# Mixing tile 0 rounded, subtracted and half multiplied inside the latent stage of a hybrid encoder layer

## What is computed

```
ret_out = silu(rg) * groupnorm(retention(q, k, v))            # 8 heads x 64
mla_out = latent_attention(...)                                # 4 heads x 128
mix = concatenate([ret_out, mla_out], axis=-1)                 # (S, 1024)
x = x + einsum('bse,ed->bsd', mix, w_out)
x = x + hier_moe(rmsnorm(x, g_ffn), ...)   # top-1 of 4 groups, top-2 of 8 experts in it
y = rmsnorm(x, g_final)
```

## Time and profile before

| what | value |
|---|---|
| three runs | 1511.76, 1516.46, 1519.86 us |
| profiled execution, its own time | 1517.54 us |
| its span, first to last instruction | 1516.0 us |
| TensorE matmuls busy | 1401.2 us (92% of the span) |
| VectorE busy | 1085.1 us (72%) |
| ScalarE busy | 859.0 us (57%) |
| GpSimd busy | 391.7 us (26%) |
| mean granted clock of TensorE | 0.968 |
| data moved | 329.12 MB, 217 GB/s over the span |

### The profile page before, as it was taken

How to read it: one execution, slowest core, us unless ns; L and a number is a source line. 1 busy time by engine, 2 the same in 40 slices (tenths; PEclk the granted TensorE clock), 3 DMA queues, 4 the chain that set the end, 5 groups by cost and what they waited for, 6 DMA issues and landing times.

```text
span 1516.0 us, 23099 instructions
## 1 busy us (share of the span) xinstructions
PE 1401.2 (92%) x8472; PEld 1159.0 (76%) x8472; DVE 1085.1 (72%) x1526; ACT 859.0 (57%) x1029; POOL 391.7 (26%) x280
## 2 busy tenths in 40 slices
PE   5999899999988999996999769999999999999983
PEld 4788788888877788885888648888887777777771
DVE  4766776444457677772576678999988888888876
ACT  5644444333446555552444457777777777777764
POOL 2000111111133000000122232666643333334431
PEclk9999999999999999998999869999999999999997
DMA  8344422222121100014557548999999999999977
GB/s 275 113 158 144 151 83 72 83 84 84 63 84 50 56 29 29 29 42 155 189 213 277 192 180 320 391 384 393 389 391 383 384 367 372 370 381 378 377 275 294
DMA packets 63242, 329.12 MB, mean 217 GB/s; under 512 B 11862, under 2 KB 18406, under 8 KB 50882
## 3 DMA queue, kind: packets, MB, share of 16 engines
q1 hardware_dynamic: 45906, 278.60, 48.5%
q0 software_dynamic: 17264, 49.56, 10.8%
HBM read 285.06 MB, written 51.80 MB: 222 GB/s over the span
## 4 chain that ended last, share of the span: by engine, by line
PE 30%; DMA 14%; issue 4%; ACT 3%; DVE 3%; POOLq 0%; DVEq 0%; POOL 0%; SPq 0%; ACTq 0%
PE acc L96 9%; PE acc L98 9%; PE acc L97 9%; DMA plain<-in_w_gate 7%; DMA odd_gate<-in_w_gate 6%; ACT shared L1825 3%; PE acc L2470 1%; PE acc L2020 1%; PE acc L2440 1%; DMA s_h_rows<-plain 1%; DVE split L1830 1%; PE acc L2031 1%; DVE plain L2605 1%; DVE plain L2643 0%; DMA plain<-s_h_rows,plain 0%
## 5 line engine op out<-in xcount | busy, mean ns | idle before, releaser
L96 PE MATMUL acc<-shared,split 128*128 128x512 f32 x952 | 383.5, 403 | 16.0 <-DVE split L2088 10.3
L98 PE MATMUL acc<-shared,split 128*128 128x512 f32 x952 | 374.7, 394 | 0.0
L96 PEld LDWEIGHTS acc<-shared,split 128*128 128x128 f32 x952 | 181.3, 190 | 53.5 <-DVE split L2088 10.6
L1830 DVE TENSOR_TENSOR even_lo<-plain,shared 128x4096 fp32r<-128x4096 f32 x48 | 211.8, 4420 | 7.8 <-ACT shared L1825 6.6
L98 PEld LDWEIGHTS acc<-shared,split 128*128 128x128 f32 x952 | 180.9, 190 | 39.0
L96 PE MATMUL pa<-shared,a_xT_hi 128*128 128x512 f32 (+1 forms) x480 | 193.2, 403 | 16.0 <-DVE a_w_lo L736 14.9
L1825 ACT CAST shared<-plain 128x4096 fp32r<-128x4096 f32 x48 | 174.3, 3633 | 40.2 <-DMA plain<-in_w_up 15.9
L98 PE MATMUL pa<-shared,a_xT_lo 128*128 128x512 f32 (+1 forms) x480 | 186.7, 389 | 0.0
L97 PE MATMUL acc<-even_lo,split 128*128 128x512 f32 x384 | 150.7, 392 | 0.0
L1830 DVE TENSOR_TENSOR split<-odd_rest,shared 128x4096 fp32r<-128x4096 f32 x31 | 137.0, 4421 | 6.0 <-ACT shared L1825 5.8
L2335 POOL DMA_INDIRECT plain<-s_h_rows,plain x32 | 133.2, 4162 | 21.9 <-issue 12.2
(11 more groups left out here) (334 smaller groups left out, 2722.6 us busy)
## 6 DMA issues: line engine op xcount, KB each, us to landing
plain<-in_w_gate SPq DMA_DIRECT2D x16, 2048.0 KB
plain<-in_w_up SPq DMA_DIRECT2D x16, 2048.0 KB
plain<-in_w_down SPq DMA_DIRECT2D x16, 2048.0 KB
odd_rest<-in_w_down SPq DMA_DIRECT2D x16, 2048.0 KB
odd_gate<-in_w_gate SPq DMA_DIRECT2D x16, 2048.0 KB, 20.5
odd_rest<-in_w_up SPq DMA_DIRECT2D x16, 2048.0 KB, 21.3
a_x_turned<-in_x_turned SPq DMA_DIRECT2D x24, 512.0 KB, 3.5
a_x_row<-in_x SPq DMA_DIRECT2D x12, 512.0 KB, 4.9
```

Of the source, the lines that this page charges most:

```text
L96: pe.matmul(out, st_hi, mv_hi, start=first, stop=False)
L98: return pe.matmul(out, st_lo, mv_hi, start=False, stop=last)
L1830: eng.tensor_tensor(self.w_lo[half][m], self.raw[half][m][:, 0:4096], self.w_hi[m].bitcast(F32), ALU.subtract).then_inc(self.s_wlo[m], 1)
```

## The change

Tile 0 of the mixing stage is begun in the latent stage. An object `Ahead` holds places and semaphores that both programs use; its semaphores are not cleared between them.

- SyncE, after the load of output piece 3, waits for the first four stores and fetches `mixT[0]` and `x[0]`; ahead of the store of group 10 it fetches `mixT[1]`.
- GpSimd, once the scores of unit 39 are made, rounds `mixT[0]` and subtracts.
- TensorE makes half 0 of tile 0 in bank 6: pieces 4 to 7, 0 and 1 (18 matmuls) after the transposes of unit 45, pieces 2 and 3 (6 matmuls) before the last weighing. `split_mix(3)` moves ahead of unit 47's rounding on ScalarE and of its subtraction on VectorE.
- SyncE no longer waits for the stores at the end of the program; the wait is ahead of the fetch of tile 2 in the mixing stage.
- The mixing stage starts with half 1 of tile 0 (24 matmuls), without a wait. The addition of x for tile 0 is in two pieces of 512 columns. Tile 1's rounding and subtraction come first on ScalarE and VectorE.

```diff
+class Ahead:
+    def __init__(self, space, sem):
+        self.mx = [space.words("f_mx0", Space.ROPE, D), space.words("f_mx1", Space.TABS, D)]
+        self.xr = space.words("f_xr", Space.KEYS + 4 * TOK, D)
+        self.hi, self.lo = space.rounded("f_hi", Space.Q_HI, D), space.rounded("f_lo", Space.Q_LO, D)
+        self.product = space.bank(6)
...
@@ phase_latent, sync @@
             load_out(3)
+            for i in range(2):
+                sp.wait_ge(s_ost[i], 32)
+            sp.wait_ge(lat.s_rst, 16 * TILES)
+            sp.wait_ge(s_rot, 6)
+            sp.dma_start(ahead.mx[0], mixT[0]).then_inc(ahead.s_in[0], 16)
+            sp.wait_ge(s_clo, TILES)
+            sp.dma_start(ahead.xr, x_all[0]).then_inc(ahead.s_xr[0], 16)
             keep_out(5)
...
             load_out(7)
+            sp.wait_ge(s_s, 40)
+            sp.dma_start(ahead.mx[1], mixT[1]).then_inc(ahead.s_in[1], 16)
             keep_out(10)
             keep_out(11)
-            sp.wait_ge(s_ost[0], 16 * NG_ // 2)
-            sp.wait_ge(s_ost[1], 16 * NG_ // 2)
@@ gpsimd @@
             pool.wait_ge(lat.s_rst, 16 * TILES)
+            pool.wait_ge(s_s, 40)
+            pool.wait_ge(ahead.s_in[0], 16)
+            nc.gpsimd.tensor_copy(ahead.hi, ahead.mx[0]).then_inc(ahead.s_mhi, 1)
+            pool.wait_ge(ahead.s_mhi, 1)
+            nc.gpsimd.tensor_tensor(ahead.lo, ahead.mx[0], ahead.hi.bitcast(F32), ALU.subtract).then_inc(ahead.s_mlo, 1)
@@ tensor @@
+            def mix_first(ks):
+                for k in ks:
+                    if k == HM:
+                        pe.wait_ge(ahead.s_mlo, 1)
+                        pe.wait_ge(s_flo, 8)
+                    elif k < HM:
+                        pe.wait_ge(s_olo, HM + k + 1)
+                    rows = slice(k * P, (k + 1) * P)
+                    three_passes(pe, pz[:], ahead.hi[:, rows], ahead.lo[:, rows], out_piece(shared, OUT_HI, k, 0),
+                                 out_piece(shared, OUT_LO, k, 0), k == HM, k == HM - 1)
...
-                if u == NU - 2:
+                if u == NU - 3:
+                    mix_first((4, 5, 6, 7, 0, 1))
+                elif u == NU - 2:
                     weigh_last(0)
+            mix_first((2, 3))
             weigh_last(1)
@@ scalar @@
                 elif u == NU - 2:
                     split_mix(2)
+                    split_mix(3)
...
-            split_mix(3)
             take_out(NG_ - 1)
@@ phase_mix, sync @@
-            sp.dma_start(mx[:, 0, :], mixT[0]).then_inc(s_in[0], 16)
-            sp.dma_start(xr[:, 0, :], x_all[0]).then_inc(s_xr[0], 16)
...
                     if t:
+                        if t == 1:
+                            for i in range(2):
+                                sp.wait_ge(ahead.s_ost[i], 96)
                         sp.wait_ge(s_mlo, t)
-                    sp.dma_start(mx[:, 1 - half, :], mixT[t + 1]).then_inc(s_in[1 - half], 16)
-                    if t:
+                        sp.dma_start(mx(t + 1, 1 - half), mixT[t + 1]).then_inc(s_in[1 - half], 16)
                         sp.wait_ge(s_x2, t)
@@ tensor @@
-            for b in range(2):
-                project(0, 0, b, range(KD))
+            for k in range(KD):
+                rows = slice(k * P, (k + 1) * P)
+                ins = three_passes(pe, po[0][:, 512:1024], ahead.hi[:, rows], ahead.lo[:, rows],
+                                   out_piece(shared, OUT_HI, k, 1), out_piece(shared, OUT_LO, k, 1), k == 0, k == KD - 1)
+            ins.then_inc(s_po, 1)
             pe.wait_ge(s_const, 112)
@@ scalar @@
-            split(0, 0, 0)
             split(1, 0, 1)
@@ vector @@
-            split(0, 0)
+            split(1, 1)
             dve.wait_ge(s_const, 112)
...
             dve.wait_ge(s_tab[1], 16)
-            split(1, 1)
...
+                if isinstance(t, int) and t == 0:
+                    nc.vector.tensor_tensor(x2[:, 0, 0:512], ahead.product, ahead.xr[:, 0:512], ALU.add)
+                    nc.vector.tensor_tensor(x2[:, 0, 512:D], po[0][:, 512:D], ahead.xr[:, 512:D], ALU.add).then_inc(s_x2, 1)
```

More of the change, by code:

```diff
@@ L1105, in phase_latent @@
         s_pt, s_phi, s_plo = sem("pt"), sem("phi"), sem("plo")
-        s_o, s_oev, s_ost = sem("o"), sem("oev"), [sem("ost0"), sem("ost1")]
+        s_o, s_oev, s_ost = sem("o"), sem("oev"), ahead.s_ost
         groups = [(0, h, 0) for h in range(HM)] + [(1, h, b) for h in range(HM) for b in (1, 2)]
@@ L1831, in lower, with phase_mix @@
                           ALU.subtract).then_inc(self.s_wlo[m], 1)
-def phase_mix(nc, block, sems, shared, split, plain, acc, ex, mixT, x_all, g_ffn, w_rg, w_re, ident_d, route_d, blocks_d, x_mid,
+def phase_mix(nc, block, sems, shared, split, plain, acc, ex, ahead, mixT, x_all, g_ffn, w_rg, w_re, ident_d, route_d, blocks_d, x_mid,
               h_rows, table, s_tick, s_tock, w_exp):
@@ L1845, in phase_mix, with mx, xr @@
         x2, h_sb = place.at([P, 2, D], F32, 48 * KB), place.at([P, 2, D], F32, 56 * KB)
-        mx, xr = place.at([P, 2, D], F32, 64 * KB), place.at([P, 2, D], F32, 72 * KB)
+        mx_places, xr_places = place.at([P, 2, D], F32, 64 * KB), place.at([P, 2, D], F32, 72 * KB)
+        def mx(t, half):
+            return ahead.mx[1] if isinstance(t, int) and t == 1 else mx_places[:, half, :]
+        def xr(t, half):
+            return ahead.xr if isinstance(t, int) and t == 0 else xr_places[:, half, :]
         hT = place.at([P, D], F32, 80 * KB)
@@ L2050, in split @@
                 act.wait_ge(s_po, t - 1 if not isinstance(t, int) else max(0, t - 1))
-                nc.scalar.copy(mT_hi[:, half, :], mx[:, half, :]).then_inc(s_mhi, 1)
-            split(0, 0, 0)
+                nc.scalar.copy(mT_hi[:, half, :], mx(t, half)).then_inc(s_mhi, 1)
             split(1, 0, 1)
@@ L2728, in build @@
         shared = ctx.enter_context(nc.sbuf_tensor("shared", [P, SHARED_WORDS], F32R))
+        later = phase_sems(nc, ctx)
         with ExitStack() as first:
@@ L2734, in build @@
             lat = Latent(nc, space, mid, d["w_cat"], lambda name: phase_sem(nc, sems, "c_" + name))
+            ahead = Ahead(space, lambda name: phase_sem(nc, later, "f_" + name))
             block = first.enter_context(nc.Block())
@@ L2738, in build @@
                                  d["w_cat"])
-            phase_latent(nc, block, sems, space, lat, d["w_out"], mixT, *rest)
+            phase_latent(nc, block, sems, space, lat, ahead, d["x"], d["w_out"], mixT, *rest)
         w_exp = [d[n].rearrange("e (p k) n -> e p (k n)", p=P) for n in ("w_gate", "w_up", "w_down")]
-        sems = phase_sems(nc, ctx)
+        sems = later
         split_base = (nc.sbuf_base + 31) // 32 * 32
@@ L2753, in build @@
         s_normed, count_blocks, enter_last, entered = phase_mix(
-            nc, block, sems, shared, split, plain, acc, ex, mixT, d["x"], d["g_ffn"], d["w_rg"], d["w_re"], d["ident"],
+            nc, block, sems, shared, split, plain, acc, ex, ahead, mixT, d["x"], d["g_ffn"], d["w_rg"], d["w_re"], d["ident"],
             d["route"], d["blocks"], x_mid, h_rows.rearrange("(t p) n -> t p n", p=P), table, s_tick, s_tock, w_exp)
```

16 lines of the change are left out of this document (9 added, 7 removed).

## The result

Four runs of the changed kernel have a median of **1505.87 us** (1503.83 to 1507.58), four of the kernel before 1516.74 us (1511.76 to 1519.86). The ratio is 0.9929, with a 95% interval of 0.9906 to 0.9951: 0.7% faster, and clear of no change. The profiled execution took 1506.92 us, its span is 1505.1 us (1516.0 before) and its mean granted clock 0.974 (0.968 before).

A forecast was written before the change was run, and what follows sets the result against it. TensorE, busy for 92% of the span, was taken as the bound, with 29.4 us around the programs' seam to rebuild. The five terms sum to 18.05 us, 11.4 less, so 1516.46 becomes 1505.1 us; range 1499 to 1512.

The forecast's parts named there:

- tail later: End of the latent stage: with the added matmuls, the last weighing ends 0.9 us later; bounds 0.5 earlier to 2.5 later.
- GpSimd holds VectorE: Latent stage near 636 us: GpSimd's copy delays a VectorE multiply by 1.0 us, TensorE loses 0.3; bounds 0 and 4.0.
- last matmul to release: Seam between the programs: without SyncE's store wait, 4.7 us becomes 2.9; bounds 2.7 and 4.8.
- release to tile 1's first matmul: Start of mixing: tile 1's matmuls wait for the constants until 8.5 us after the release; nearer bounds 6.2 and 8.9.
- its 24 matmuls: Start of mixing: the 24 matmuls of tile 1's first half take 5.45 us, at 0.227 us each.
- It hardly matters, because of the next wait: Start of mixing: the first 24 matmuls take 5.45, 7.2 or 8.4 us by clock, hidden behind the constants' 8.5 us.
- B: Rival, chance 0.13: half is saved; GpSimd costs 3.7 us more, a clock fall awaiting constants 2.7; 5.0 us gained, 1511.5.
- A: Rival, chance 0.14: more is saved; constants land 6.2 us after the release, saving 13.7 us, giving 1502.8 us.
- C: Rival, chance 0.07: expert weights' transfers run at their own pace from a fixed moment, so the end stays at 1516.5 us.
- D: Rival, chance 0.06: slower; GpSimd's rounding copy is long and holds VectorE; at 20 us for both operations, 1524 us.

The follow-up runs named there:

- the repeated change: The changed kernel run once more, unaltered: median 1505.71 us, ratio 0.9935 to the kernel before.
- the copy put on a multiply: Against the changed kernel, GpSimd's pair also waits for s_peak, meant to start its copy just ahead of a VectorE multiply; one execution took 1506.37 us.
- tile 1's fetch in mixing: Against the changed kernel, tile 1's mixing row is fetched first in the mixing stage, ahead of the constants; one execution took 1506.80 us.
- twice: Against the changed kernel, GpSimd rounds and subtracts tile 0 a second time, after unit 43's scores; median 1511.18 us, ratio 0.9962 to the kernel before.
- half 0 in mixing: Against the changed kernel, tile 0's half 0 (24 matmuls) is back in the mixing stage; median 1512.26 us, ratio 0.997 to the kernel before.
- the store's wait kept: Against the changed kernel, SyncE again waits for all twelve stores at the first program's end; median 1509.11 us, ratio 0.9949 to the kernel before.

## Why the prediction was right, and where it was not

The forecast was 1505.1 us, the median is 1505.87. The sum behind it was 18.05 us in place of 29.4. Its five terms, in the profile of after:

| term | predicted | measured | read from |
|---|---|---|---|
| tail later | 0.9 | 0.57 | 14.66 - 14.09 |
| GpSimd holds VectorE | 0.3 | 3.72 | A, 45.57 - 41.85 |
| last matmul to release | 2.9 | 2.83 | 690.52 to 693.35 |
| release to tile 1's first matmul | 8.5 | 7.78 | 693.35 to 701.13 |
| its 24 matmuls | 5.45 | 5.37 | 701.13 to 706.50 |
| sum | 18.05 | 20.27 | |

So the stretch gave 9.1 us and not 11.4. The span nevertheless fell by 10.9, because the program up to unit 36 happened to be 1.5 us shorter and D 0.2. **The number came out closer than its working deserved**, by luck; the mechanism was right, the size of one term was not. In the repeated change, without the fall of the clock in A, the three stretches gave 10.3 us.

**The tail: right.** 18 matmuls filled the idleness before unit 46's transposes, and the clock was 1.00 there. The last weighing waited for VectorE, 0.23 us. The net value of the move, 3.7 us between two profiles, was measured with half 0 put back.

**GpSimd beside VectorE: this step failed.** The term of 0.3 us measured 3.72, and 2.08 where the clock did not fall. The prediction said that the copy would hold up the multiply of 635.96 by 1.0 us, of which TensorE takes 0.7 without loss. Three things in it were wrong. First, the copy was given the subtraction's 2.35 us for want of a row, and took 1.04; so it was over before the multiply came, and the subtraction stood in its place, 0.10 us ahead of it. Second, the 0.7 us of slack did not exist. VectorE was the one that set the pace: TensorE waited for take_lo, which stands behind the multiply there (the wait of 638.01 ends with c_pT_lo), and the starts of two multiplies moved from 3.19 us apart (635.96 to 639.15) to 5.27 (634.43 to 639.70), the whole 2.08 us. The smaller hold of the copy put on a multiply says the same: 0.74 us held, 0.77 lost in A. Third, TensorE idled for 1.78 us, and the prediction had priced no fall of the clock in the latent stage; it cost another 1.6 us in the profiles of after and of tile 1's fetch in mixing. The Trainium skill ("SBUF — State Buffer", section "Who interferes with whom") says that the one that comes second waits for the other's whole instruction; the rows of after (2.83 us) and of the copy put on a multiply (1.53 and 1.49 us) agree in both directions to about 0.2 us, the overlaps being 2.29, 0.62 and 0.93 us and the delays 2.08, 0.49 and 0.74. It also says that on trn2 reductions don't take part, nor VectorE operations with at most one SBUF input outside the modes that use both of its ports; the reduction's 1.21 and the subtraction's 1.28 us, unchanged, agree. The prediction quoted that rule and yet sized the term by the copy alone. Against multiplies that come 3.2 us apart, the subtraction could have been given a meeting of its own, at most its length, 2.35 us by the earlier trace rows (an estimate of the bound). The row of 476.30 fits less well than the prediction has it: there GpSimd's start is recorded 0.02 us behind the multiply's, and yet the multiply was held. Which of two comes first can't be told from starts so close.

**The seam: right.** 2.83 us, and the wait that was taken away returned as 1.95 us when it was put back.

**The start of mixing: right in kind, 0.7 us too dear.** The constants were late next, as the sum said, but 7.76 us after the release. They were faster than the 8.9 us of before: w_re's transfer was issued in 0.66 us instead of 2.08, and 1 MB no longer stood ahead of them. The clock was low at the start, as the prediction left open: 0.53 in the window 695 to 697 and 1.00 from 697. The first 24 matmuls still ended at 700.7, 0.42 us before the constants, so they did hide behind them. In the repeated change they did not: the low clock lasted 6.0 us, the 24 matmuls took 8.43 us, and they were late next, not the constants. "It hardly matters, because of the next wait" held in the profile of after, and cost 0.7 us in the repeated one.

**The rivals.** Half of B came true, and that in size only: its 3.7 us for GpSimd were both operations held in full, and the 3.72 measured are one held multiply, 2.08 us, and a fall of the clock, 1.6. The other half did not: the wait for the constants was 0.42 us and no fall followed it. One did in "twice", where that wait was 2.20 us. A did not come true, since the constants took 7.76 us and not 6.2. C falls with the 10.5 us by which the first expert transfer came earlier, D with the copy's 1.04 us.

## What to carry to other kernels

When idle GpSimd is given work, look not at its slack but at what VectorE does in those microseconds: a subtraction of two SBUF operands holds a VectorE multiply by a scalar for its whole length, and one wait more on GpSimd, for a signal behind which VectorE reads PSUM or does something else, removes that. At a seam, sum up what every engine waits for and then ask of each wait which instruction is the first that needs it; in the profile of after the constants were ready 5.6 us before their first use on TensorE and still cost it a stop of 0.42 us. And compare stretches between marks that both kernels have: a span that agrees with the forecast can hold two errors that cancel.

## What the runs showed of the hardware

- Idleness of 1.78 us on TensorE was followed by a fall of the granted clock to 1.2 GHz in two profiles (after, and tile 1's fetch in mixing) and not in four (the repeated change, twice, half 0 in mixing, the store's wait kept), with the same instructions around it. It costs 1.6 us when it comes. The 1.99 us ahead of unit 46's transposes were followed by one in both profiles that have them (before, and half 0 in mixing). A difference of that size between two single profiles can be this alone.
- On GpSimd a rounding copy of 128x1024 took 1.04 us and a subtraction of the same size 2.38 to 2.41 us.
- SyncE's issue of one small constant (in_blocks) took 2.64 us in the chain of after, and 3.92 us with one more tile's fetch ahead of it. In the chain of after the five issues ahead of it took 0.34 to 0.67 us and the one behind it 1.03. Before, both w_re (2.08) and in_blocks (2.44) were long. Why these was not tried.
- The part of the program behind tile 0's transposes, whose code hardly differs, took between 795.2 and 798.5 us in the profiles of the changed versions. What moves it stays open, and so does that share of the difference in the medians.
